# Reciprocals of the softmax row sums: turned to rows by two small transfers per head through DRAM instead of transposes on TensorE

## The reference, cut to what matters

```python
s = q @ k.T * scale            # fox: + cum[t] - cum[s]
s = where(key_pos <= query_pos, s, -inf)
p = softmax(s, axis=-1)        # exp(s - max) / sum
o = p @ v                      # v: (L, 64)
```

## Time and the profile before

| | us |
|---|---|
| median of 3 runs | 1492.43 (1490.75 to 1493.87) |
| the profiled execution, its own time | 1491.13 |
| its span, first to last instruction | 1489.2 |
| TensorE busy in the span | 1466.7 |
| VectorE, ScalarE, GpSimd busy | 840.2, 695.8, 53.1 |

### The profile page before, as it was taken

How to read it: one execution, slowest core, us unless ns; L and a number is a source line. 1 busy time by engine, 2 the same in 40 slices (tenths; PEclk the granted TensorE clock), 3 DMA queues, 4 the chain that set the end, 5 groups by cost and what they waited for, 6 DMA issues and landing times.

```text
span 1489.2 us, 26616 instructions
## 1 busy us (share of the span) xinstructions
PE 1466.7 (98%) x11503; PEld 1296.0 (87%) x11503; DVE 840.2 (56%) x1237; ACT 695.8 (47%) x1041; POOL 53.1 (4%) x150
## 2 busy tenths in 40 slices
PE   7999999999999999999999999999999999999998
PEld 7999999999999989898888777788899888878888
DVE  6487977764656665662435787542223666643343
ACT  6565868843342322232323766532223776743232
POOL 0000000000000000000000121000000111100000
PEclk9999999999999999999999999999999999999999
DMA  7222222133322322322235200222332111123221
GB/s 242 86 85 67 79 66 64 53 96 136 111 85 99 101 85 86 113 85 96 83 98 116 34 30 1 86 85 85 100 98 63 57 57 57 57 85 100 85 96 74
DMA packets 134871, 126.04 MB, mean 85 GB/s; under 512 B 24521, under 2 KB 132836, under 8 KB 134500
## 3 DMA queue, kind: packets, MB, share of 16 engines
q1 hardware_dynamic: 134084, 120.39, 25.2%
q0 software_dynamic: 656, 3.96, 0.9%
q10 hardware_dynamic: 16, 0.00, 0.0%
HBM read 119.69 MB, written 4.26 MB: 83 GB/s over the span
## 4 chain that ended last, share of the span: by engine, by line
PE 91%; DVE 4%; ACT 3%; issue 1%; DMA 0%; SPq 0%; DVEq 0%; ACTq 0%
PE PS L908 78%; PE PS L1245 2%; PE PS L1190 2%; PE PS L1212 2%; DVE wlo L1906 1%; PE PS L1195 1%; PE PS L1196 1%; PE PS L1019 1%; ACT L1399 1%; ACT whi L1399 0%; PE PS L1197 0%; PE PS L1222 0%; DMA xt<-in_x 0%; PE PS L975 0%; PE PS L1075 0%
## 5 line engine op out<-in xcount | busy, mean ns | idle before, releaser
L908 PE MATMUL PS<-zhi,whi 128*128 128x258 f32 (+2 forms) x1856 | 488.3, 320 | 3.0 <-ACT hT L1399 1.4
L908 PE MATMUL PS<-zhi,wlo 128*128 128x258 f32 (+2 forms) x1856 | 476.2, 314 | 0.0
L908 PE MATMUL PS<-zlo,whi 128*128 128x258 f32 (+2 forms) x1856 | 475.3, 314 | 0.6 <-DVE zlo L1954 0.6
L908 PEld LDWEIGHTS PS<-zhi,whi 128*128 128x128 f32 x1856 | 306.8, 189 | 28.0 <-issue 1.9
L908 PEld LDWEIGHTS PS<-zhi,wlo 128*128 128x128 f32 x1856 | 305.5, 189 | 22.1
L908 PEld LDWEIGHTS PS<-zlo,whi 128*128 128x128 f32 x1856 | 305.0, 188 | 20.1 <-DVE zlo L1954 0.8
L1906 DVE TENSOR_TENSOR wlo<-raw,whi 128x2048 fp32r<-128x2048 f32 (+2 forms) x114 | 247.8, 2174 | 115.7 <-ACT whi L1399 115.5
L1399 ACT ACTIVATE whi<-raw 128x2048 fp32r<-128x2048 f32 (+2 forms) x114 | 207.4, 1820 | 142.9 <-DMA raw<-in_w_up 54.2
L1399 ACT ACTIVATE Pm<-PS,small 128x144 f32<-128x144 f32 (+3 forms) x128 | 68.8, 540 | 46.3 <-DVE small L2466 45.4
L2466 DVE TENSOR_REDUCE small<-PS 128x1 f32<-128x144 f32 (+3 forms) x128 | 63.4, 504 | 38.1 <-PE PS L1197 36.6
L908 PE MATMUL PS<-ghi,whi 128*128 128x512 f32 x176 | 69.6, 396 | 0.0
(11 more groups left out here) (362 smaller groups left out, 2118.4 us busy)
## 6 DMA issues: line engine op xcount, KB each, us to landing
raw<-in_w_in SPq DMA_DIRECT2D x50, 1024.0 KB, 5.0
raw<-in_w_up SPq DMA_DIRECT2D x22, 1024.0 KB, 5.0
raw<-in_w_out SPq DMA_DIRECT2D x8, 1024.0 KB, 4.8
raw<-in_w_down SPq DMA_DIRECT2D x8, 1024.0 KB, 4.7
raw<-in_w_br_mla SPq DMA_DIRECT2D x4, 1024.0 KB, 4.7
raw<-in_w_br_fox SPq DMA_DIRECT2D x4, 1024.0 KB, 4.8
raw<-in_w_down SPq DMA_DIRECT2D x4, 768.0 KB, 4.2
hspill<-hT SPq DMA_DIRECT2D x1, 2112.0 KB, 7.5
```

The costliest lines, as they stand in the source:

```text
L908: ins = mm(o_, l_, r_, start=first, stop=last)
```

## The change

The reciprocals of head `x` no longer pass TensorE. `rinv` gets eight columns, four for each head of a pair. GpSimd issues two transfers per head. `turn_root(x)` writes the 128x4 reciprocals to a row of 512 in DRAM (`rq`), each run one number of 4 bytes. `spread_root(x)` waits until that has landed and reads the row into 64 partitions of `rs` (64 runs of 2048 bytes). They stand in `gather_ends` between the `Pe` copies of the next head, the first behind the copy of block 0 and the second behind that of block 1; for the last head they stand alone. `rs` becomes two tiles that take turns by pair. `turn_sums`, the spreading copy with its `settle`, the copy by ScalarE, and `r_turned` and `r_copied` with the waits on them go; VectorE's product waits for `r_in` in their place. 

```diff
-                for h in range(HEADS):
+                def turn_root(x):
+                    pool.wait_ge(A.r_ready, x + 1)
...
+                        nc.gpsimd.dma_start(A.rq[x].rearrange("(i c) -> c i", i=QB),
+                                            rinv[:, 4 * (x % 2):4 * (x % 2) + 4]).then_inc(A.r_out, 16)
+                def spread_root(x):
+                    pool.wait_ge(A.r_out, 16 * (x + 1))
+                    if x:
+                        pool.wait_ge(A.r_in, 16 * x)
+                    if x >= 4:
+                        pool.wait_ge(A.o_ready, x // 2 - 1)
+                    nc.gpsimd.dma_start(A.rs[x // 2 % 2][64 * (x % 2):64 * (x % 2) + 64, :],
+                                        A.rq[x:x + 1, :].broadcast_to([64, SEQ])).then_inc(A.r_in, 16)
+                for h in range(HEADS + 1):
+                    if h == HEADS:
+                        turn_root(h - 1)
+                        spread_root(h - 1)
+                        break
...
                     for i in range(QB):
+                        if h and i == 1:
+                            turn_root(h - 1)
+                        elif h and i == 2:
+                            spread_root(h - 1)
                         pool.wait_ge(A.p_exp, 4 * h + i + 1)
...
-                    if h and h % 2 == 0:
-                        pe.wait_ge(A.r_copied, h // 2)
...
-            def turn_sums(A, p):
-                pe.wait_ge(A.r_ready, 2 * p + 2)
-                pe.wait_ge(A.pt_a, 4 * p + 4)
-                for i in range(QB):
-                    ins = tr(PS[:, 2, P * i:P * (i + 1)], A.rx[:, i, :], ident[:, :])
-                ins.then_inc(A.r_turned, 1)
...
-                        turn_sums(A, h // 2 - 1)
                         weigh(A, h // 2 - 1)
...
-                                act.wait_ge(A.r_turned, p + 1)
-                                if p:
-                                    act.wait_ge(A.o_ready, p)
-                                A_(A.rs[:, :], PS[:, 2, :], ACT.Copy).then_inc(A.r_copied, 1)
...
                                 if x >= 2:
-                                    dve.wait_ge(A.r_turned, x // 2)
+                                    dve.wait_ge(A.r_out, 16 * (x - 1))
...
-                                tick(V.reciprocal(rinv, rowsum[:, s:s + 4]))
-                                settle()
-                                V.tensor_copy(A.rx[:, :, DV * (x % 2):DV * (x % 2) + DV],
-                                              rinv.unsqueeze(2).broadcast_to([P, QB, DV])).then_inc(A.r_ready, 1)
+                                V.reciprocal(rinv[:, s:s + 4], rowsum[:, s:s + 4]).then_inc(A.r_ready, 1)
...
-                                dve.wait_ge(A.r_copied, p + 1)
-                                V.tensor_tensor(omla[:, p, :], PS[:, 7, :], A.rs[:, :], ALU.mult).then_inc(A.o_ready, 1)
+                                dve.wait_ge(A.r_in, 32 * (p + 1))
+                                V.tensor_tensor(omla[:, p, :], PS[:, 7, :], A.rs[p % 2][:, :], ALU.mult)\
+                                 .then_inc(A.o_ready, 1)
```

More of the change, by code:

```diff
@@ L443, in build_program @@
         trig, e = at("trig", [P, 3, T], F32, e)
-        rxm, e2 = at("rxm", [P, QB, P], F32, e)
-        rsm, e2 = at("rsm", [P, SEQ], F32, e2)
+        rsm0, e2 = at("rsm0", [P, SEQ], F32, e)
+        rsm1, e2 = at("rsm1", [P, SEQ], F32, e2)
         r1, e2 = at("r1", [P, SEQ], F32, e2)
@@ L449, in build_program @@
         nch, _ = at("nch", [P, T], F32R, e)
-        rsf, _ = at("rsf", [P, SEQ], F32, e)
+        rsf0, _ = at("rsf0", [P, SEQ], F32, e)
         e += T * 4
@@ L472, in build_program @@
         assert e2 <= MIXOFF
-        rxf, _ = at("rxf", [P, QB, P], F32, N0 + 4 * T * 4)
+        rsf1, _ = at("rsf1", [P, SEQ], F32, N0 + 4 * T * 4)
         mtok, _ = at("mtok", [P, QB, D], F32, C + 16384)
@@ L480, in build_program @@
         lb, omlb, lbe, epst, fbias = small[:, 8:16], small[:, 16:24], small[:, 24:40], small[:, 40:41], small[:, 41:42]
-        negmax, rowsum, rinv, ssum, lbt = small[:, 48:56], small[:, 56:64], small[:, 64:68], small[:, 72:76], small[:, 80:96]
+        negmax, rowsum, rinv, ssum, lbt = small[:, 48:56], small[:, 56:64], small[:, 64:72], small[:, 72:76], small[:, 80:96]
         fsum, g12 = small[:, 96:112], small[:, 112:120]
@@ L565, in build_program, with __init__ @@
         class Attn:
-            def __init__(self, name, rx, rs):
-                self.rx, self.rs = rx, rs
+            def __init__(self, name, rs):
+                self.rs = rs
+                self.rq = nc.dram_tensor(name + "rq", [HEADS, SEQ], F32, kind="Internal").ap()
                 self.s_done, self.m_ready = sem(name + "s_done"), sem(name + "m_ready")
                 self.p_exp, self.r_ready = sem(name + "p_exp"), sem(name + "r_ready")
-                self.r_turned, self.r_copied = sem(name + "r_turned"), sem(name + "r_copied")
+                self.r_out, self.r_in = sem(name + "r_out"), sem(name + "r_in")
                 self.g_turned, self.pt_a, self.pt_v = sem(name + "g_turned"), sem(name + "pt_a"), sem(name + "pt_v")
@@ L573, in __init__ @@
                 self.e_ready, self.v_moved = sem(name + "e_ready"), sem(name + "v_moved")
-        mla, fox = Attn("mla_", rxm, rsm), Attn("fox_", rxf, rsf)
+        mla, fox = Attn("mla_", (rsm0, rsm1)), Attn("fox_", (rsf0, rsf1))
         hspill = nc.dram_tensor("hspill", [P, KT * T], F32, kind="Internal").ap()
@@ L795, in gather_ends @@
             def gather_ends(A):
-                for h in range(HEADS):
+                def turn_root(x):
+                    pool.wait_ge(A.r_ready, x + 1)
+                    with nc.allow_non_contiguous_dma(reason="four reciprocals of each query's partition turned to a row"):
+                        nc.gpsimd.dma_start(A.rq[x].rearrange("(i c) -> c i", i=QB),
[13 more added lines that the diff above has]
+                        break
                     if h >= 2:
@@ L1308, in _ @@
             pe.wait_ge(mla.pt_v, 2 * HEADS)
-            pe.wait_ge(mla.r_copied, KT)
             pe.wait_ge(z2_lo, KT)
@@ L1377, in _ @@
             pe.wait_ge(fox.pt_v, 2 * HEADS)
-            pe.wait_ge(fox.r_copied, KT)
             for k in range(3, KT):
@@ L1731, in attention @@
                         if i == 1:
-                            if h >= 3 and h % 2 == 1:
-                                p = h // 2 - 1
-                                act.wait_ge(A.r_turned, p + 1)
-                                if p:
-                                    act.wait_ge(A.o_ready, p)
-                                A_(A.rs[:, :], PS[:, 2, :], ACT.Copy).then_inc(A.r_copied, 1)
-                            elif A is mla and h >= 2:
+                            if A is mla and h >= 2 and h % 2 == 0:
                                 k = h // 2 - 1
```

## The result

The changed kernel takes 1590.34 us (median of 4 runs, 1586.65 to 1594.34) against 1492.57 for the one before: 1.0657 times as long, 95% interval 1.0642 to 1.0672. That is 98 us slower where 7 us faster was forecast.

The account below looks back on a forecast made before the run. TensorE, busy 98% of the span, was taken as the bound. Removed transposes gave -7.1 us, ScalarE's and VectorE's removed copies and the added transfers nothing: 1492.4 - 7.1 = 1485.3 us, range 1482.5 to 1489.5.

Parts of the forecast that it names:

- the turning transfer: On GpSimd's queue, 512 runs of 4 bytes to DRAM: forecast to land in 2.9 us, ends 2.2 and 5.3.
- The spreading transfer: On GpSimd's queue, 128 KB in 64 runs into `rs`: forecast at 2.5 us, making 5.4 for the two transfers.
- The limits: Second head of a pair in `mla`: TensorE stops only if the two transfers take over 8.9 us together.
- The slow rival: Transfers late at VectorE's product in `mla`, excess over 8.9 us lost five times; +7.4 us, 1499.8; chance 0.12.
- The copies of blocks 2 and 3: GpSimd's copies behind the first landing's wait: 1 to 2 us later, needed over 6 us later, cost nothing.
- 12.3 us to spare: In `fox`: the reciprocal is needed 12.3 us later, over all ends of the two transfers, so no wait.
- The gain itself: Four transposes per pair removed from TensorE, 16 pairs: 7.1 us at 0.44 each, up to 8.5 at 0.53.
- The pair period: Sign of being right, in `mla`: down from 14.70 to 14.26 us, and by the same 0.44 in `fox`.
- the removed work of ScalarE and VectorE: 16 ScalarE and 32 VectorE copies, some 19 us busy time, counted at nothing because TensorE's stream covers them.
- The rival in which another wait takes the gain: TensorE reaches exponentials or `PT` copies sooner and waits there; four fifths of gain lost, 1491.0; chance 0.07.
- GpSimd's lock: VectorE copies may delay GpSimd or its descriptors; up to 2.3 us in odd iterations of `fox`, costing nothing.
- the row of loads: Stretch of 12480 packets averaging 168 bytes: 15.5 ns each, kept as the price of the turning transfer's 512 runs.

Follow-up runs that it names:

- e6: The kernel before with one unread transfer per head beside it, six shapes of run length, spacing and direction taking turns, GpSimd waiting for each; 1493.47 us against 1491.31.
- e3: The changed kernel with the turning transfer, still 512 runs of 4 bytes, issued from ScalarE's hardware queue; 1591.32 us, ratio 1.067.
- e2: The changed kernel with the row laid out by pairs of blocks, 256 runs of 8 bytes; 1486.92 us against 1491.31 before, ratio 0.9972.
- e1: The changed kernel with the row laid out query by block, 128 runs of 16 bytes, product reading with a stride; 1486.54 us against 1492.73 before, ratio 0.9956.
- e4: The kernel before with unread 512-run turning transfers beside it, GpSimd waiting for each landing, no product waiting; 1521.28 us, 29 more than before.
- The ceiling: The changed kernel without both transfers and their waits, product multiplied by ones; 1486.05 us (ratio 0.9962), and again 1486.15 (0.9956).
- e8: The kernel before with 30 unread, unwaited turning transfers of 128 runs of 16 bytes beside it; 1491.41 us against 1492.27, ratio 0.9996.
- e5: The kernel before with unread 512-run turning transfers of 4-byte runs beside it, GpSimd not waiting for their landing; 1503.7 us.

## Why the prediction was wrong

**The step that failed** is the turning transfer. I put it at 2.9 us, with ends of 2.2 and 5.3, and it took 9.4. I took the price of 512 runs from a stretch of short packets, 15.5 ns each, and allowed for no more than the slowest landing of a few single numbers. Both rows are loads into SBUF. The prediction says that no row shows 4-byte writes to DRAM, and then sets a high end from the other direction all the same. e6 shows how far apart the two are: 2.5 us into SBUF, 8.5 into DRAM. The 15.5 ns are not contradicted; packets were over in 2 us in e3. What followed them had no term in my sum.

**The spreading transfer** was put at 2.5 us. It took 4.1 and 4.8 in the changed kernel, where turning transfers were about, and 2.9 to 3.3 beside 16-byte runs. The two together were 13.5 us in `mla` and 14.2 in `fox`, in place of 5.4.

**The limits.** TensorE was to stop when the two take over 8.9 us. The cases on either side agree: 6.6 us (e2) and some 4.7 (e1) cost nothing, 13.5 cost much.

**The slow rival** was the right one, late transfers at the product's wait, with the right victim behind it, group 3 behind VectorE's copy of group 1. It was given 0.12, and its price was far too small. By its formula 13.5 us would cost 5 x (13.5 - 8.9) - 7.1 = +16 us; it was +98. It also counted five pairs of `mla`, and seven stopped TensorE. Three things were missing.

First, GpSimd's queue. The copies of blocks 2 and 3 behind its wait were counted at nothing; once a head takes GpSimd longer than it takes TensorE, that queue falls behind at every head, and e4 shows 29 us for it alone, without a product that waits.

Second, `fox`, which I had cleared with 12.3 us to spare. The two transfers take 14.2 us there in the median, which is over 12.3 by itself. In four of its eight pairs GpSimd issued the turning transfer within 0.7 us of the second head's reciprocal, and the row was late all the same; in the other four it issued 4.7 to 5.5 us late, as it was still waiting for the head before. One pair of the first kind, 13.3 us from the issue to the product:

```profile
1282.78 0.17 DVE L2483 RECIPROCAL small<-small 128x4 f32<-128x4 f32 x1
1283.51 0.79 POOL L802 DMA_DIRECT2D fox_rq<-small  x1 [0.27 <-issue]
...
1296.83 0.69 DVE L2489 TENSOR_TENSOR omla<-PS,rsf 128x512 f32<-128x512 f32 x1 [1.46 <-DMA rsf<-fox_rq]
```

Third, the clock: some 28 us of slower matmuls in and behind the stops had no term.

**What held.** The gain itself: 7.1 us (up to 8.5) forecast for the transposes. The ceiling gave back 5.3 (1491.31 to 1486.05) and 6.1, and e1 6.2. The pair period was to go from 14.70 to 14.26 us; in e1 the product starts at 871.84 and at 886.09 in the chain, 14.25 apart:

```profile
871.84 2.31 PE PS L1262 x16
...
886.09 2.30 PE PS L1262 x16
```

The remaining 1 us or so of the 7.1 lies in which executions the medians are made of. At a granted clock of 1.000 the kernel before took 1491.1 us (mean of four) and the ceiling beside it 1484.1 (one), and the second time 1490.9 (one) and 1484.3 (mean of two): 7.0 and 6.6 us, from few executions. The difference between executions isn't the change's: the profiled one of the ceiling lost 1.7 us to a lower clock from 176 to 181 us, far ahead of the attentions, and so did that of e8, which keeps the transposes, while that of the kernel before has no such stretch there. That the removed work of ScalarE and VectorE is worth nothing is in line with the ceiling, which had it removed too. The rival in which another wait takes the gain did not come. Of the two rules of the Trainium skill that were weighed, the one about GpSimd's lock (SBUF — State Buffer, Who interferes with whom) changed nothing that these runs show. The other (DMA: Bandwidth & Descriptors, Specifications), that below 512 bytes the engines read, change and write back, spoke against the change, and I let the row of loads outvote it. As it stands it doesn't give the answer either: runs of 16 bytes, and of 4 bytes 64 apart, are under 512 as well and land in 2.2 and 2.7 us.

**What stays open.** Where behind the packets the 6 us go, in the memory or in the engines' write side, no run tells. Only distances of 4 and 64 bytes were tried for single words, so the size of the piece that the writes share isn't known either, nor whether it matters that they come from different partitions: no run wrote neighbouring words as separate runs from one partition.

## What to carry to other kernels

When columns are turned into a row by a transfer through DRAM, lay the row out so that what one partition holds stays one run, and let the reader take the stride: 128 runs of 16 bytes landed in 1.7 us and cost about 1 us or nothing, 512 runs of 4 bytes took 9.4 and cost 98 us. A price read from loads is no bound for stores, and a wait in a queue that serves every head must be compared with the period of a head, not only with the one deadline. Before a transfer goes behind a saturated TensorE, reckon a stop at more than its length, as the granted clock was at half speed for 5 us behind a stop of 4.

## What was not expected of the hardware

- Neighbouring 4-byte words written to DRAM by different runs: 8.5 us for 512 of them and 7.5 for 128, against 2.7 with 64 bytes between them.
- GpSimd's software queue and ScalarE's hardware queue were equally slow at it, 9.4 and 8.9 us. In the transfer shown on ScalarE's queue (e3) the packets were over within 2 us, and some 7 us passed without any until the semaphore.
- Transfers under way beside it were held too. A weight load took 16.1 us (e5) and 16.7 (the changed kernel), where 8.8 was the longest before, and a spreading transfer 10.1, where 3.4 was the longest in e1.
- Reading the spread row with a stride of 16 bytes made VectorE's product of 128x512 take 1.07 us in place of 0.69; a stride of 8 bytes did not. It cost the kernel nothing that the intervals show.
